# Two feed-forward blocks: one 512-column product for both operand parts, and the two halves of the bank added afterwards

## The reference, cut to what matters

```python
def conv_ffn(xn, w_gate, conv_w, conv_b, w_up, w_down):
    g = xn @ w_gate                              # 256 x 1024 times 1024 x 2816
    gp = jnp.pad(g, ((0, 0), (CONV_WIDTH - 1, 0), (0, 0)))
    gc = conv_b + sum(conv_w[j] * gp[:, j:j + S] for j in range(CONV_WIDTH))
    h = jax.nn.gelu(gc, approximate=False) * (xn @ w_up)
    return h @ w_down
...
h = h + mix
f = conv_ffn(rms_norm(h, norm_ffn[i]), ...)      # i = 0 and 1
h = h + f
```

## Time and profile before

| | before |
|---|---|
| median of 3 runs | 1076.24 us (1076.22 to 1076.35) |
| span of the profiled execution | 1074.6 us |
| time outside the span, against the median | 1.6 us |
| TensorE busy | 1066.0 us (99%) |
| VectorE busy | 721.0 us (67%) |
| ScalarE busy | 575.9 us (54%) |
| mean granted TensorE clock | 1.00 |

### The profile page before, as it was taken

How to read it: one execution, slowest core, us unless ns; L and a number is a source line. 1 busy time by engine, 2 the same in 40 slices (tenths; PEclk the granted TensorE clock), 3 DMA queues, 4 the chain that set the end, 5 groups by cost and what they waited for, 6 DMA issues and landing times.

```text
span 1074.6 us, 19953 instructions
## 1 busy us (share of the span) xinstructions
PE 1066.0 (99%) x8108; PEld 951.9 (89%) x8108; DVE 721.0 (67%) x1230; ACT 575.9 (54%) x977; POOL 141.7 (13%) x166
## 2 busy tenths in 40 slices
PE   9999999999999999999999999999999999999998
PEld 7887878656898999799999999999997899999997
DVE  4665566387554878768875676666776776766674
ACT  4532676544444467866665464444564555445454
POOL 0000010253200001532432000000023310000000
PEclk9999999999999999999999999999999999999999
DMA  9731121286613432057444365555533334555551
GB/s 382 318 137 67 73 79 40 98 287 213 229 40 119 146 138 80 9 189 235 148 167 157 121 233 174 180 196 168 204 139 118 119 119 157 197 199 177 212 177 40
DMA packets 25387, 168.79 MB, mean 157 GB/s; under 512 B 3280, under 2 KB 3536, under 8 KB 5456
## 3 DMA queue, kind: packets, MB, share of 16 engines
q1 hardware_dynamic: 25152, 167.25, 43.9%
q10 hardware_dynamic: 144, 0.26, 0.1%
HBM read 164.35 MB, written 1.05 MB: 154 GB/s over the span
## 4 chain that ended last, share of the span: by engine, by line
PE 96%; DVE 2%; ACT 2%; issue 0%; DVEq 0%; ACTq 0%
PE bank L437 26%; PE bank L438 25%; PE bank L439 25%; PE bank L1550 2%; PE bank L494 2%; PE bank L1714 2%; PE bank L1704 2%; PE bank L1694 1%; PE bank L1577 1%; PE bank L1568 1%; PE bank L446 1%; PE bank L2363 1%; PE bank L1395 1%; DVE wlo L415 1%; ACT TILE L1753 1%; PE bank L1688 1%
## 5 line engine op out<-in xcount | busy, mean ns | idle before, releaser
L437 PE MATMUL bank<-OPH,whi 128*128 128x256 f32 (+1 forms) x1716 | 519.7, 303 | 0.3
L439 PE MATMUL bank<-OPH,wlo 128*128 128x256 f32 (+1 forms) x1716 | 511.2, 298 | 0.0
L438 PE MATMUL bank<-OPL,whi 128*128 128x256 f32 (+1 forms) x1716 | 511.2, 298 | 0.0
L415 DVE TENSOR_TENSOR wlo<-raw,whi 128x1024 fp32r<-128x1024 f32 (+1 forms) x255 | 304.2, 1235 | 102.6 <-ACT whi L400 102.5
L437 PEld LDWEIGHTS bank<-OPH,whi 128*128 128x128 f32 x1716 | 328.0, 191 | 17.3 <-issue 5.2
L438 PEld LDWEIGHTS bank<-OPL,whi 128*128 128x128 f32 x1716 | 328.2, 191 | 10.0 <-issue 1.2
L439 PEld LDWEIGHTS bank<-OPH,wlo 128*128 128x128 f32 x1716 | 328.1, 191 | 9.8
L400 ACT ACTIVATE whi<-raw 128x1024 fp32r<-128x1024 f32 (+1 forms) x255 | 255.2, 1051 | 74.6 <-PE bank L439 72.1
L437 PE MATMUL bank<-whi,OPH 128*128 128x256 f32 (+2 forms) x272 | 93.8, 345 | 0.2 <-DVE OPL L717 0.2
L438 PE MATMUL bank<-wlo,OPH 128*128 128x256 f32 (+2 forms) x272 | 91.2, 335 | 0.0
L439 PE MATMUL bank<-whi,OPL 128*128 128x256 f32 (+2 forms) x272 | 91.1, 335 | 0.0
(11 more groups left out here) (291 smaller groups left out, 1136.6 us busy)
## 6 DMA issues: line engine op xcount, KB each, us to landing
raw<-in_stream SPq DMA_DIRECT2D x143, 1024.0 KB, 4.9
PROJ<-in_stream SPq DMA_DIRECT2D x5, 1024.0 KB, 18.8
raw<-in_stream SPq DMA_DIRECT2D x4, 1056.0 KB, 8.6
PROJ<-PROJ SPq DMA_DIRECT2D x32, 64.0 KB, 3.9
FIRST<-in_first SPq DMA_DIRECT2D x1, 1248.0 KB, 6.0
C<-in_con SPq DMA_DIRECT2D x1, 1157.5 KB, 7.3
FIRST<-in_first SPq DMA_DIRECT2D x1, 1024.0 KB, 8.1
WST<-in_w_s SPq DMA_DIRECT2D x2, 256.0 KB, 7.3
```

The costliest lines, as they stand in the source:

```text
L415: nc.vector.tensor_tensor(c.w[1][:, part], c.raw[:, part], c.w[0][:, part].bitcast(F32), ALU.subtract).then_inc(*raises(c.lo[h]))
L437: nc.tensor.matmul(out, w[0], x[0], start=start, stop=False, skip_group_check=skip)
L438: nc.tensor.matmul(out, w[0], x[1], start=False, stop=False, skip_group_check=skip)
L439: return nc.tensor.matmul(out, w[1], x[0], start=False, stop=stop, skip_group_check=skip)
```

## The change

OPH and OPL become the two planes of one tile OPS, side by side for each k. For gates and ups, a new helper issues one matmul of whi with both planes (512 columns: the rounded part in the bank's first half, the remainder in its second), and one of wlo with OPH into the first half. A half t now fills a whole bank: each gate takes banks 2 and 3, each up banks 0 and 1. ScalarE copies the two second halves out, and VectorE adds them to the first halves; the product with the factor is then made in SBUF.

```diff
-        OPH, OPL = sb("OPH", [P, KD, T], F32R), sb("OPL", [P, KD, T], F32R)
+        OPS = sb("OPS", [P, KD, 2, T], F32R)
+        OPH, OPL = OPS[:, :, 0, :], OPS[:, :, 1, :]
...
+        def products_apart(bank, w, k, lo, start, stop):
+            both = bank[:].rearrange("p (a b) -> p a b", b=SEQ)
+            nc.tensor.matmul(both, w[0], OPS[:, k, :, lo:lo + SEQ], start=start, stop=False, skip_group_check=True)
+            return nc.tensor.matmul(bank[:, 0:SEQ], w[1], OPH[:, k, lo:lo + SEQ], start=False, stop=stop,
+                                    skip_group_check=True)
...
-                g.append(GBANK.take("pe", ("dve",)))
-                up.append(GBANK.take("pe", ("dve",)))
+                g.append([b.take("pe", ("dve",)) for b in banks[2:4]])
+                up.append([b.take("pe", ("dve",)) for b in banks[0:2]])
...
+            def wide(e, us, ch):
+                for point in due(e, ch.lo):
+                    e.wait_ge(*point)
+                for t, u in enumerate(us):
+                    for point in due(e, u.empty):
+                        e.wait_ge(*point)
                     for k in range(KD):
+                        mm = products_apart(u.mem, cols(ch, k, t * P, P), k, lo, k == 0, k == KD - 1)
+                    mm.then_inc(*raises(u.full))
+
+            def copy_halves(e, what, c, us, both):
+                for point in due(e, us[0].full, us[1].full, ("halves_summed", l, c - 1, what) if c else None):
+                    e.wait_ge(*point)
+                nc.scalar.activation(part[what], both[:, :, SEQ:2 * SEQ], ACT.Copy).then_inc(
+                    *raises(("low_copied", l, c, what)))
+
+            def add_halves(e, what, c, out, both):
+                for point in due(e, ("low_copied", l, c, what)):
+                    e.wait_ge(*point)
+                nc.vector.tensor_tensor(out, both[:, :, 0:SEQ], part[what], ALU.add).then_inc(
+                    *raises(("halves_summed", l, c, what)))
...
                     split_hi(e, by["gate", c].s + (3 if c else 4))
+                    copy_halves(e, "gate", c, g[c], g_both)
...
                     nc.scalar.activation(t1[c].mem[:], t1[c].mem[:], ACT.Gelu).then_inc(*raises(("gelu_made", l, c)))
+                    copy_halves(e, "up", c, up[c], up_both)
...
-                    nc.vector.tensor_tensor(pad[c % 2][:, :, 2:SEQ + 2], two(g[c].mem), rr, ALU.mult).then_inc(*raises(("gate_scaled", l, c)))
+                    padded = pad[c % 2][:, :, 2:SEQ + 2]
+                    add_halves(e, "gate", c, padded, g_both)
+                    for point in due(e, ("halves_summed", l, c, "gate"), ("factor_made", f"ffn{l}")):
+                        e.wait_ge(*point)
+                    nc.vector.tensor_tensor(padded, padded, rr, ALU.mult).then_inc(*raises(("gate_scaled", l, c)))
...
-                    nc.vector.tensor_tensor(two(t2[c].mem), two(up[c].mem), rr, ALU.mult).then_inc(*raises(up[c].read["dve"]))
+                    add_halves(e, "up", c, two(t2[c].mem), up_both)
+                    for point in due(e, ("halves_summed", l, c, "up")):
+                        e.wait_ge(*point)
+                    nc.vector.tensor_tensor(two(t2[c].mem), two(t2[c].mem), rr, ALU.mult).then_inc(*tick("dve"))
+                    e.wait_ge(*ticked("dve"))
...
-                g[c].freed[:] = [("gate_scaled", l, c)]
+                for i in range(2):
+                    g[c][i].freed[:] = [("halves_summed", l, c, "gate")]
+                    up[c][i].freed[:] = [("halves_summed", l, c, "up")]
```

More of the change, by code:

```diff
@@ L2831, in ffn @@
             g, up, t1, t2 = [], [], [], []
+            g_both, up_both = twin[1], twin[0]
+            part = {what: PROJ[:, at:at + 512].rearrange("p (a b) -> p a b", b=SEQ)
+                    for what, at in (("gate", 9224), ("up", 9736))}
             for c in range(NF):
-                g.append(GBANK.take("pe", ("dve",)))
-                up.append(GBANK.take("pe", ("dve",)))
+                g.append([b.take("pe", ("dve",)) for b in banks[2:4]])
+                up.append([b.take("pe", ("dve",)) for b in banks[0:2]])
                 t1.append(tile.take("act", ("dve",)))
                 t2.append(tile.take("dve", ("act", "dve")))
-                by["gate", c].used, by["up", c].used = g[c].full, up[c].full
+                by["gate", c].used, by["up", c].used = g[c][1].full, up[c][1].full
                 by["down", c].used = ("down_added", l, c)
@@ L2843, in ffn @@
             rr = r.unsqueeze(1).broadcast_to([P, 2, SEQ])
-            def wide(e, u, ch):
-                for point in due(e, u.empty, ch.lo):
+            def wide(e, us, ch):
+                for point in due(e, ch.lo):
                     e.wait_ge(*point)
-                for t in range(2):
+                for t, u in enumerate(us):
+                    for point in due(e, u.empty):
+                        e.wait_ge(*point)
                     for k in range(KD):
[L2850 to L2854, removed]
+                        mm = products_apart(u.mem, cols(ch, k, t * P, P), k, lo, k == 0, k == KD - 1)
[10 more added lines that the diff above has]
+                    *raises(("halves_summed", l, c, what)))
             def narrow(e, c, ch):
@@ L2896, in pe @@
                 for k in range(KD):
-                    for u, ch in both:
-                        for point in due(e, u.empty, ch.lo[k // 4], op_block(k)):
+                    for us, ch in both:
+                        for point in due(e, [u.empty for u in us], ch.lo[k // 4], op_block(k)):
                             e.wait_ge(*point)
[L2900 to L2904, removed]
+                        for t, u in enumerate(us):
+                            mm = products_apart(u.mem, cols(ch, k, t * P, P), k, lo, k == 0, k == KD - 1)
+                            if k == KD - 1:
+                                mm.then_inc(*raises(u.full))
                 total.add(e)
@@ L2929, in act @@
                                                   bias=vec("conv_b", 22 * l + j + b),
[L2930 removed]
+                                                  scale=vec("conv_w", 66 * l + 44 + j + b)).then_inc(*raises(("newest_tap", l, c) if b else ("newest_tap", l, c, "half")))
                     split_hi(e, by["up", c].s + 3)
@@ L2953, in dve @@
                     split_lo(e, by["gate", c].s + (3 if c else 4))
-                    for point in due(e, g[c].full, ("factor_made", f"ffn{l}"), ("pads_zeroed", l, c % 2)):
+                    for point in due(e, ("pads_zeroed", l, c % 2)):
                         e.wait_ge(*point)
@@ L2968, in dve @@
                             if tap:
-                                ins.then_inc(*raises(("older_tap", l, c, b)))
+                                ins.then_inc(*raises(("conv_done", l, c, "older", b)))
                             else:
-                                ins.then_inc(*raises(("conv_done", l, c) if b else ("conv_half_done", l, c)))
+                                ins.then_inc(*raises(("conv_done", l, c) if b else ("conv_done", l, c, "half")))
                         if tap:
-                            e.wait_ge(*when(("older_tap", l, c, 1)))
+                            e.wait_ge(*when(("conv_done", l, c, "older", 1)))
                     split_lo(e, by["up", c].s + 3)
-                    for point in due(e, up[c].full, t2[c].empty):
+                    for point in due(e, t2[c].empty):
                         e.wait_ge(*point)
-                    nc.vector.tensor_tensor(two(t2[c].mem), two(up[c].mem), rr, ALU.mult).then_inc(*raises(up[c].read["dve"]))
-                    for point in due(e, ("gelu_made", l, c), up[c].read["dve"]):
+                    add_halves(e, "up", c, two(t2[c].mem), up_both)
[3 more added lines that the diff above has]
+                    e.wait_ge(*ticked("dve"))
+                    for point in due(e, ("gelu_made", l, c)):
                         e.wait_ge(*point)
@@ L3005, in ffn @@
             s.used = [("down_added", l, NF - 1)]
-            s.operand_used = [up[NF - 1].full]
+            s.operand_used = [up[NF - 1][1].full]
             return s
```

## The result

The median after is 1084.93 us (4 runs, 1084.65 to 1085.21), against 1076.30 before (1076.22 to 1076.60): a ratio of 1.0079, interval 1.0068 to 1.0091. The forecast was 1077.7 with a range up to 1083.0. The kernel is 8.6 us slower, and 1.9 us above the range.

The account below looks back on a forecast made before the run. TensorE was taken to bound the kernel, busy 1066 of 1074.6 us. The 9.4 us saved were outweighed by 10.9 of waits (ffn0 +2.09, ffn1 -0.58): +1.5, median 1077.7 us, range 1074.3 to 1083.

Parts of the forecast that it names:

- Entry: At each block's start, up 0 waits for both its banks: 0.30 us, and 0.07 for a restart.
- waits of gate 1: In each block's first part, gate 1 waits for the addition of gate 0: 3.58 us each.
- ends: TensorE waits 1.92 us between ffn0's end and the next stage, and 0.20 + 0.07 us at ffn1's end.
- Middle periods: Added copies and additions cost nothing there; h is whole 11.21 us after gate c's last matmul starts.
- The clock: The sum kept 2.4 GHz behind both 3.6 us standstills; a fall to 1.2 GHz was only a rival, chance 0.12.
- What the merging saves: In gates and ups, each pair of 256-column matmuls made one 512 saves 0.0133 us; 704 pairs, 9.4 us.
- My bounds of 0.2133 and 0.240: Merged 512-column matmul's time in us: columns alone (18.8 us saved) or nothing saved; 0.2267 was taken.
- rival 4: Slower by size: strided moving operand at 0.240 us, or longer waits; 1078.5 to 1087 us, likeliest 1079.5; chance 0.26.
- The waits before gate 2 and up 2 of ffn0: In ffn0's first part, each waits for its split, which stands behind added additions: 0.75 and 0.59 us.
- third rival: Clock falls to 1.2 GHz behind gate 1's two standstills: +3 to +11 us, 1081 to 1088; chance 0.12.
- 0.38 for slower: Chance of the whole kernel ending above the 0.2% band (1074.1 to 1078.4), against 0.50 same and 0.12 faster.

Follow-up runs that it names:

- the two filled ones: Changed kernel with 28 or 15 calls of matmuls of ones filling the standstill before gate 1 in both blocks: 1086.74 and 1083.83 us.
- the contiguous kernels: Changed kernel, 512-column matmuls from c = 1 streaming one run instead of two: 1084.97 us alternating; 1081.17 us with eight 512s, then eight 256s.
- the best order here: Kernel before with only c = 2 to 9 merged, two 512s then two 256s in turn: 1070.06 us, ratio 0.9943.

## Why the prediction was wrong, by its steps

**Entry, waits of gate 1, ends: right.** The two waits were 3.62 and 3.60 against 3.58, the end of ffn0 1.94 against 1.92. The entry came out to the hundredth in ffn0; in ffn1 it was 0.21 longer, by the pace. The rows of the engines beside them bear the working out; in the groups by form after, a copy takes 594 ns (0.60 forecast) and an addition 689:

```profile
L2869 ACT ACTIVATE PROJ<-bank 128x512 f32<-128x512 f32 x44 | 26.1, 594 | 51.8 <-PE bank L446 51.8
...
L2875 DVE TENSOR_TENSOR PROJ<-bank,PROJ 128x512 f32<-128x512 f32 x22 | 15.2, 689 | 31.1 <-ACT PROJ L2869 31.1
```

In the first part of ffn0 the copy lies under VectorE's split, and the factor follows the addition at once (ACT, then DVE after):

```profile
600.66 0.58 ACT L2869 ACTIVATE PROJ<-bank 128x512 f32<-128x512 f32 x1
```

```profile
601.41 0.68 DVE L2875 TENSOR_TENSOR PROJ<-bank,PROJ 128x512 f32<-128x512 f32 x1
602.12 0.69 DVE L2986 TENSOR_TENSOR PROJ<-PROJ,KDUP 128x512 f32<-128x512 f32 x1
```

**Middle periods: right.** TensorE has no wait in them. With its last matmul of gate c at about 660.4, the timeline of DVE has the remainder of h at 670.91 + 0.69, which is G + 11.2 as worked out:

```profile
661.50 0.69 DVE L2875 TENSOR_TENSOR PROJ<-bank,PROJ 128x512 f32<-128x512 f32 x1 [1.98 <-ACT PROJ L2869]
...
670.91 0.69 DVE L3015 TENSOR_TENSOR OPS<-TILE,OPS 128x512 fp32r<-128x512 f32 x1 [0.70 <-ACT OPS L2962]
```

**The clock: the step that failed first.** I had the standstills to a tenth and the fall of the clock as a rival at 0.12, and the sum went on at 2.4 GHz. All six traces with unfilled standstills of 3.6 us show 0.50 behind both of them, the two filled ones 1.00: shown, not argued. The sum had put the lower clock at nothing. It cost 4.35 us, two thirds of it at gate 1, and some 2.9 net of the waits that it hid. The rival had +3 to +11 us with the right mechanism, without the fall behind ffn0. That the measured time lies within its 1081 to 1088 is in part luck, since the pace brought more of the difference than the clock did. The Trainium skill ("TensorE: Matmul & The Clock Gate", part 1) has the clock fall after TensorE has idled, and the traces agree, 0.50 in all three places. I had cited it and weighed it by the absence of such a gap in the trace before, which is no evidence against it: that trace could not show it.

**What the merging saves: the term that was mis-sized.** 0.0133 a pair was taken from streams in which all matmuls have one width. In the alternating stream it was mostly 0.0067, some 5 us in all instead of 9.4. The earlier trace rows came from the middle of a run of 512s; the trace of before also has 512s directly behind 256s, in ffn1, and there the first five take (1059.54 - 1058.38) / 5 = 0.232 each, not 0.2267, at which a pair saves 0.008 (timeline of PE, first and sixth):

```profile
1058.38 0.40 PE L437 MATMUL bank<-whi,OPH 128*128 128x512 f32 x1
...
1059.54 0.39 PE L439 MATMUL bank<-whi,OPL 128*128 128x512 f32 x1
```

So the rows on hand could have warned that a mixed stream has another price. My bounds of 0.2133 and 0.240 held it (0.2367 + 0.1167 is the same as 0.2333 beside 0.120), and rival 4 named it for another reason, a strided operand; the contiguous kernels show that the stride costs nothing. With the clock alone put right the sum would have given about 1080.6 us, with the pace alone about 1082.1, both inside the range: it took the two together to leave it. The Trainium skill (the same page, the section on 56 ns) has 2.5 ns for each matmul saved, 1.8 us in all, and would put the change at about 1085, the measured time, but for the wrong reason: the pairs gain 0.0121 in the best order here, and the time was lost to the clock too.

**The waits before gate 2 and up 2 of ffn0: absent.** 0.75 and 0.59 were forecast, and none is in the trace, since TensorE itself was late by the clock. With the clock held both come back, at 0.58 and 0.44. Two losses on one path do not add, which the prediction had noted in its third rival.

Chances: 0.38 for slower was too little. The two lapses, a known mechanism left out of the sum and a price from the nearest row carried to a mixed stream, both moved the time the same way.

## What to carry to other kernels

A change that trades matmuls for passes on other engines pays where the periods have slack, here c = 2 to 9, and is to be left out at the block's start and end, where the order of the work leaves none. When a sum contains a standstill of TensorE of some 3.6 us, put the lower clock behind it into the sum, and then subtract the waits it hides. The price of each matmul is to be read from a stream of the same mix of widths, or at least from the place where one width follows the other, and the order in which equal work is issued is worth a test of its own.

## What of the hardware was not expected

A stream of alternating 512 and 256 columns ran at 0.3467 or at 0.3533 us a pair within one kernel; two of each gave 0.3482 and eight of each 0.3493, and streams of one width 0.120 and 0.2267. Behind 256s the first five 512s take 0.232 on average. A standstill at the end of ffn0 (idle time of 1.6 to 1.8 us) lowered the clock in 4 of the 8 traces that have it; what decides between them stays open. Idle time of 3.3 us at gate 1 lowered it in all 12 places where it was left unfilled, in six traces. In one of them it fell only 1.4 us after TensorE had started again. And the matmuls of ones were two passes a call, twice what I had sized them for.
